# Second half of the memory gate's product in a float32 decoder layer: four of its eight weight pieces as seven block products each, with their sums on VectorE

## The reference

```python
h = rmsnorm(x, g_pre_mix[l])
proj = h @ w_in[l]
q_in, ckv, k_rope, lru_x, lru_y, gate_mla, gate_lru = jnp.split(proj, IN_SPLIT_IDX, axis=-1)
o_mla = mla_attention(q_in, ckv, k_rope, positions, g_ckv[l], w_ukv[l]) @ w_o_mla[l]
...
merged = jax.nn.sigmoid(gate_mla) * o_mla + jax.nn.sigmoid(gate_lru) * o_lru
```

## Time and profile before

| | |
|---|---|
| median of 3 runs | 1704.6 us (1704.03 to 1705.01) |
| the profiled execution's own time | 1704.42 us |
| its span, first to last instruction | 1702.6 us |
| TensorE matmul (PE) busy | 1694.0 us, 99%, 8887 matmuls |
| TensorE weight load (PEld) busy | 1453.7 us, 85% |
| VectorE (DVE) busy | 1293.3 us, 76% |
| ScalarE (ACT) busy | 980.3 us, 58% |
| GpSimd (POOL) busy | 266.5 us, 16% |
| chain that ended last | PE 97%, DVE 1%, ACT 1% |
| DMA | 375 MB, mean 220 GB/s |

### The profile page before, as it was taken

One profiled execution on the slowest core, in us unless ns is written; L12 is line 12 of the kernel. 1 busy time (PEld: TensorE's weight loads), 2 busy tenths in 40 slices (PEclk: granted clock), 3 DMA queues, 4 the chain that ended last, 5 costly groups with the idle time before them and its releaser, 6 DMA issues.

```text
span 1702.6 us, 24583 instructions
## 1 busy us (share of the span) xinstructions
PE 1694.0 (99%) x8887; PEld 1453.7 (85%) x8887; DVE 1293.3 (76%) x1638; ACT 980.3 (58%) x1238; POOL 266.5 (16%) x340
## 2 busy tenths in 40 slices
PE   9999999999999999999999999999999999999998
PEld 8888888888888888888888888888888888888887
DVE  7766675468788897676897687778877778977787
ACT  7656655454577766455556575556555555545564
POOL 0012212211365540002011101110001110001100
PEclk9999999999999999999999999999999999999999
DMA  9644459998678758499699856556765556765555
GB/s 346 204 132 149 152 188 293 316 268 237 177 221 232 234 175 301 133 368 274 234 302 255 220 198 196 183 184 208 253 199 178 181 195 212 236 201 191 197 187 203
DMA packets 230873, 375.07 MB, mean 220 GB/s; under 512 B 8720, under 2 KB 165008, under 8 KB 228752
## 3 DMA queue, kind: packets, MB, share of 16 engines
q1 hardware_dynamic: 210992, 326.66, 57.1%
q0 software_dynamic: 13888, 32.51, 9.4%
q10 hardware_dynamic: 5920, 14.94, 2.3%
HBM read 369.89 MB, written 36.70 MB: 239 GB/s over the span
## 4 chain that ended last, share of the span: by engine, by line
PE 97%; DVE 1%; ACT 1%; issue 1%; POOL 1%; DVEq 0%; ACTq 0%; POOLq 0%
PE ps L637 48%; PE ps L712 30%; PE ps L959 8%; PE ps L651 3%; PE ps L804 2%; PE ps L942 1%; PE ps L868 1%; PE ps L774 1%; PE ps L763 0%; ACT wsp L1629 0%; PE ps L744 0%; PE ps L897 0%; PE ps L873 0%; PE ps L1341 0%; PE ps L683 0%
## 5 line engine op out<-in xcount | busy, mean ns | idle before, releaser
L2010 DVE TENSOR_TENSOR wsp<-raw,wsp 128x2048 fp32r<-128x2048 f32 (+2 forms) x304 | 674.0, 2230 | 186.7 <-ACT wsp L1406 163.4
L1406 ACT ACTIVATE wsp<-raw 128x2048 fp32r<-128x2048 f32 (+2 forms) x274 | 502.1, 1843 | 126.4 <-PE ps L712 96.7
L637 PE MATMUL ps<-asp,wsp 128*128 128x512 f32 x3032 | 529.0, 336 | 0.0
L637 PEld LDWEIGHTS ps<-asp,wsp 128*128 128x128 f32 x3032 | 463.4, 188 | 62.8 <-DVE asp L2605 0.3
L712 PE MATMUL ps<-wsp,hsp 128*128 128x512 f32 x1536 | 354.0, 390 | 0.0
L712 PEld LDWEIGHTS ps<-wsp,hsp 128*128 128x128 f32 x1536 | 287.6, 188 | 59.7
L637 PE MATMUL ps<-hsp,wsp 128*128 128x512 f32 (+1 forms) x1744 | 314.1, 338 | 0.0
L637 PEld LDWEIGHTS ps<-hsp,wsp 128*128 128x128 f32 x1744 | 268.1, 188 | 36.7
L712 PE MATMUL ps<-wsp,asp 128*128 128x512 f32 x768 | 175.1, 389 | 0.0
L1417 ACT ACTIVATE cr<-ps 128x256 f32<-128x256 f32 x185 | 69.4, 380 | 180.9 <-PE ps L637 159.8
L712 PEld LDWEIGHTS ps<-wsp,asp 128*128 128x128 f32 x768 | 144.0, 188 | 29.8
(11 more groups left out here) (336 smaller groups left out, 1555.1 us busy)
## 6 DMA issues: line engine op xcount, KB each, us to landing
raw<-in_w_up SPq DMA_DIRECT2D x88, 1024.0 KB, 5.4
raw<-in_w_in SPq DMA_DIRECT2D x56, 1024.0 KB, 5.4
raw<-in_w_in SPq DMA_DIRECT2D x32, 768.0 KB, 4.5
raw<-in_w_down SPq DMA_DIRECT2D x24, 1024.0 KB, 5.4
sums<-in_w_down POOLq DMA_DIRECT2D x76, 256.0 KB, 7.5
raw<-in_w_o_mla SPq DMA_DIRECT2D x16, 1024.0 KB, 10.3
raw<-in_w_o_lru SPq DMA_DIRECT2D x16, 1024.0 KB, 6.1
raw<-sums SPq DMA_DIRECT2D x31, 512.0 KB, 3.9
```

Of the source, the lines that this page charges most:

```text
L637: mm = pe.matmul(ps[:, bank, 0:w], lhs(part, k), x[:, 0:w], start=(f and part == 0), stop=(l and part == 1))
L1406: act.activation(wsp[:, p0 % SLOTS, 0, 0:n], raw[:, p0 % SLOTS, 0:n], ACT.Copy).then_inc(hi_done, 1)
L2010: dve.tensor_tensor(wsp[:, slot, 1, 0:n], raw[:, slot, 0:n], wsp[:, slot, 0, 0:n].bitcast(F32), ALU.subtract).then_inc(lo_done, 1)
```

## The change

The second half becomes a phase of its own with twelve pieces (`GM_PLAN`): four plain ones as before (S0, S1, S6, S11), and four pairs "first", "made" for row blocks 8 to 15: (S2, S3), (S4, S5), (S7, S8), (S9, S10). A pair takes two row blocks k, k + 1 of 128 rows, both halves of the tokens and both halves of the columns, which is a 2 by 2 by 2 block product of eight block multiplications, and does it as seven (Winograd's form of Strassen's scheme). Seven by three terms are 21 matmuls of 128 x 512: 9 on "first", 12 on "made".

- SyncE loads the four weight blocks of a pair in three DMAs: two for "first" (768 KB), one of 256 KB for "made".
- VectorE makes the four weight sums of a pair itself (`gm_sums`, four additions of 128 x 512), then the low part of "first" (128 x 1536), later that of "made" (128 x 2048). ScalarE makes the high part of "made" only after the sums.
- The forms of h (four blocks of 128 x 128 for each pair, in `GM_FORMS`) are made in the first half: for each of G6, G7, S0, S1, VectorE runs `gm_form_sums` (one addition of 128 x 512, four operations of 128 x 128), ScalarE the high part (`gm_form_high`) and VectorE the low part (`gm_form_low`).
- The seven products gather in banks 0 to 3, the plain ones in banks 4 to 7. Behind the last pair ScalarE copies one bank out and VectorE does four operations (`gm_products`); after the last piece VectorE adds the four plain banks (`gm_plain`), and ScalarE takes the sigmoid in SBUF.
- TensorE waits for `gm_products` before M0, since M0 writes banks 0 to 3.

The diff, cut to what is spoken of:

```diff
+GM_PLAN = [("plain", 0), ("plain", 1), ("first", 4), ("made", 4),
+           ("first", 5), ("made", 5), ("plain", 2), ("first", 6),
+           ("made", 6), ("first", 7), ("made", 7), ("plain", 3)]
...
-PH_GM = Phase(PH_Q, 2, [0, 0, 0, 2] * 2, crosses=False)
+PH_GM = [Phase(PH_Q, 1, [0, 0, 0, 2] * 2, crosses=False)]
+PH_GM.append(Phase(PH_GM[0], 1, [0] * (len(GM_PLAN) - 1) + [4], crosses=False, twice=GM_FIRST))
...
 # TensorE
+                arrive(PH_GM[1], 0, c)
+                if c == GM_FIRST[0]:
+                    pe.wait_ge(tile_out, PH_GM[0].t_end)
+                if kind == "first":
+                    pe.wait_ge(gm_form_lo, GM_LO + pair - 4 + 1)
...
+                elif kind == "first":
+                    form_mm(q1, block(k0, 0), slot, 1, c == GM_FIRST[0], c == GM_FIRST[-1])
+                    form_mm(dn_plain_bank(1, 0, 1), block(k1, 0), slot, 3, False, False)
+                    mm = form_mm(dn_plain_bank(1, 0, 0), form(3), slot, 2, False, False)
+                else:
+                    first, last = c == GM_MADE[0], c == GM_MADE[-1]
+                    form_mm(q5, form(1), slot, 0, first, last)
+                    form_mm(q7, form(0), slot, 1, first, last)
+                    form_mm(q6, form(2), slot, 2, first, last)
+                    mm = form_mm(dn_plain_bank(1, 1, 1), block(k1, 1), slot, 3, False, False)
...
+            pe.wait_ge(gm_out, GM_OUT + 4)
             enter(PH_OM, [0, 1, 2, 3])
...
 # ScalarE
+            def gm_form_high(n):
+                act.wait_ge(gm_form_raw, GM_RAWS + n + 1)
+                act.activation(GM_FORMS[:, n, :, 0, :], GM_RAW.rearrange("p (f t) -> p f t", f=4), ACT.Copy).then_inc(gm_form_hi, 1)
             for c in range(4, 8):
-                hi(PH_GM, 0, c + LEAD)
+                hi(PH_GM[0], 0, c + LEAD)
+                gm_form_high(c - 4)
             gm_gates(0, 1)
...
 # VectorE
+            def gm_sums(ph, c):
+                first, made = (raw[:, (ph.p0 + at) % SLOTS, :] for at in (c, c + 1))
+                for at in (c, c + 1):
+                    dve.wait_ge(landed[(ph.p0 + at) % SLOTS], ph.landed(0, at))
+                own.mark(dve.tensor_tensor(made[:, 512:1024], made[:, 1536:2048], first[:, 1024:1536], ALU.add))
+                own.link(dve.tensor_tensor(made[:, 0:512], made[:, 1536:2048], first[:, 512:1024], ALU.add))
+                own.link(dve.tensor_tensor(made[:, 1024:1536], made[:, 0:512], first[:, 1024:1536], ALU.add))
+                dve.tensor_tensor(made[:, 1536:2048], made[:, 1024:1536], first[:, 1536:2048], ALU.add).then_inc(sums_made, 1)
...
             for c in range(4, 8):
-                lo(PH_GM, 0, c + LEAD)
+                lo(PH_GM[0], 0, c + LEAD)
+                if c > 4:
+                    gm_form_low(c - 5)
+                gm_form_sums(c - 4)
+            for c in range(LEAD, len(GM_PLAN) + LEAD):
+                if c in GM_FIRST:
+                    gm_sums(PH_GM[1], c)
+                    first_low(PH_GM[1], c)
+                else:
+                    lo(PH_GM[1], 0, c)
+                if c == LEAD:
+                    gm_form_low(3)
+                if c == GM_MADE[-1] + 2:
+                    gm_products()
+            gm_plain()
```

More of the change, by code:

```diff
@@ L76 @@
             ("plain", 4), ("first", 5), ("made", 5), ("first", 7), ("made", 7), ("plain", 6)]]
+GM_PLAN = [("plain", 0), ("plain", 1), ("first", 4), ("made", 4),
+           ("first", 5), ("made", 5), ("plain", 2), ("first", 6),
+           ("made", 6), ("first", 7), ("made", 7), ("plain", 3)]
+GM_FIRST, GM_MADE = ([c for c, (kind, _) in enumerate(GM_PLAN) if kind == name] for name in ("first", "made"))
 WO_PLAN = [("plain", pair) for pair in range(8)] + [
@@ L712, in rows_mm, with form_mm @@
                     mm = pe.matmul(ps[:, bank, :], src[:, k, low * T + m * P:low * T + (m + 1) * P], wsp[:, c, part, cols],
+                                   start=(first and t == 0), stop=(last and t == 2))
+                return mm
+            def form_mm(bank, lhs, slot, block, first, last):
+                for t, (part, low) in enumerate(TERMS):
+                    mm = pe.matmul(ps[:, bank, :], lhs(low), wsp[:, slot, part, quarter(block)],
                                    start=(first and t == 0), stop=(last and t == 2))
@@ L918, in _ @@
+            for c in range(len(GM_PLAN)):
+                gm_piece(c)
+            for b in gm_banks:
+                last_in.pop(b, None)
+            pe.wait_ge(gm_out, GM_OUT + 4)
             enter(PH_OM, [0, 1, 2, 3])
@@ L955, in turn_merged @@
                     turn(a_tok, k, 4 + k // 2 % 4, (k % 2) * T, m_turned)
-            def form_mm(bank, lhs, slot, block, first, last):
-                for t, (part, low) in enumerate(TERMS):
-                    mm = pe.matmul(ps[:, bank, :], lhs(low), wsp[:, slot, part, quarter(block)],
-                                   start=(first and t == 0), stop=(last and t == 2))
-                return mm
             def gl_half(h):
@@ L2215, in _, with gm_plain @@
+            def gm_plain():
+                dve.wait_ge(gm_out, GM_OUT + 4)
+                for n in range(4):
+                    dve.wait_ge(gemm_step, PH_GM[1].g(0, PH_GM[1].done[n]))
+                    dve.tensor_tensor(gm_res(n), gm_res(n), ps[:, 4 + n, :], ALU.add).then_inc(gm_out, 1)
+            attention(HEADS // 2 - 1, PH_GM[0], 0, lambda part: None)
             e_, s_, s2, p_ = st[:, 48:64], st[:, 32:48], st[:, 64:80], st[:, 80:96]
```

155 lines of the change are left out of this document (114 added, 41 removed).

## The result

The changed kernel takes 1717.22 us, the median of five executions (1715.55 to 1719.5); the kernel before, beside it, 1704.6 (1704.03 to 1705.01). The ratio is 1.0075, with a 95% interval of 1.0063 to 1.0086: slower by 12.6 us. Forecast were 1712.5 and at most 1715.0. The sign was right, and the time came out above the range.

The account below looks back on a forecast made before the run. The prediction took TensorE to bound the kernel. Against the profiled 1704.42 us it summed -2.72 (matmuls saved) + 9.49 (waits for low parts) + 1.31 (S11's load) = +8.08, so 1712.5 us, range 1708.7 to 1715.0.

Parts of the forecast that it names:

- Removed work: Second half on TensorE: 60 block products in place of 64, 12 matmuls fewer, 2.72 us saved.
- The handshake in the first half: ScalarE and VectorE wait on each other over the forms: rounds of 7.20 us; S0, S1, S2 late by 1.66, 1.76, 2.01.
- The rival in which it doesn't bind: First half: the lead of 7.9 us covers the form work, only the pairs count; 1703.2 us, chance 0.09.
- The pairs: Second half: VectorE takes 6.93 us per pair, TensorE 4.76; waits at S3, S4, S5, S9, S10 of 0.55 to 1.61 us.
- The load of S11: DMA of S11's weights, slowed beside GpSimd's additions, lands at 334.6, so TensorE begins S11 late: +1.31 us.
- the first rival: S11's load is in time, as GpSimd's additions may run earlier; all else as forecast: 1711.2 us, chance 0.25.
- S8's load: Other loads of the stage were said to have 1 us or more in hand, this one the least.
- The step that failed: End of the second half: four adds and sigmoids behind S11 cost nothing, hidden by M0 and M1 (10.9 us of TensorE).
- The rival of 1718: TensorE's clock falls to 1.2 GHz at each of the three longest waits, 6 us more; chance 0.03.

Follow-up runs that it names:

- e6: e3, with GpSimd's second batch of weight sums in DRAM held until S10's matmuls are done: 1703.37 us, ratio 0.9993; repeated in another series, 1703.34 us.
- e4: The kernel before, with only the forms made in its first half in the change's order and used by nobody: 1712.38 us, ratio 1.0047.
- e2: The changed kernel, with each form's high part one place later on ScalarE, behind the next piece's high part: 1710.77 us, ratio 1.0038.
- e3: The changed kernel with the edits of e1 and e2 together: 1705.76 us, ratio 1.0005.
- e1: The changed kernel, with M0's first turn on TensorE no longer waiting for the second half's sigmoids: 1713.45 us, ratio 1.0053.
- e8: The kernel before, with one wait added: TensorE begins S1 only after the low part of S3: 1706.95 us, ratio 1.0016.

## Why the prediction was right and wrong

**Removed work: right.** 12 matmuls fewer, 2.72 us. In e6, where two small waits are left, M0 begins 1.4 us earlier: by the pace 0.56 us are lost at S9, 0.65 at S10 (both with the restart) and 0.13 behind it, and 2.72 - 1.34 = 1.38.

**The handshake in the first half: right, and it decides.** Forecast were low parts 7.20 us apart. The timeline of VectorE in the changed kernel:

```profile
285.20 2.29 DVE L2098 TENSOR_TENSOR wsp<-raw,wsp 128x2048 fp32r<-128x2048 f32 x1 [2.50 <-ACT wsp L1479]
...
292.38 2.29 DVE L2098 TENSOR_TENSOR wsp<-raw,wsp 128x2048 fp32r<-128x2048 f32 x1 [2.50 <-ACT wsp L1479]
...
299.57 2.29 DVE L2098 TENSOR_TENSOR wsp<-raw,wsp 128x2048 fp32r<-128x2048 f32 x1 [2.50 <-ACT wsp L1479]
```

And that of ScalarE:

```profile
289.92 0.63 ACT L1638 ACTIVATE gm_forms<-cr 128x512 fp32r<-128x512 f32 x1 [4.74 <-DVE cr L2331]
```

The low parts stand 7.18 and 7.19 apart. In each round VectorE waits 2.50 us for ScalarE, and ScalarE 4.74 for VectorE. e4 shows the cause without the rest of the change, and e2 removes it by an order alone. The rival in which it doesn't bind (1703.2) fell; e6's 1703.4 is its number, but by another order. A slip in the forecast's working: 192 matmuls are 43.6 us and not 43.5 (65.41 x 192 / 288), which puts S0's wait at 1.76 in place of 1.66; measured were 1.74. Another, without effect: the earlier trace rows leave out a wait of PEld of 1.5 us for `ident`, so 0.7 was not the longest in the kernel.

**The pairs: right.** 6.93 us forecast for each on VectorE, against TensorE's 4.76; from one "made" low part to the next it takes 7.0, and the waits at S3 to S5 and S10 came out within 0.1 us.

**The load of S11: wrong, and made up for by chance.** "I take 334.6" gave 1.31 us at S11; S11 lost 0.12. The additions of GpSimd were over earlier than before, as the first rival allowed: its next ones were issued at 327.99 in place of 336.13, and S11's load, issued at 326.76, took 5.0 us. Instead the weights of S7 came late for VectorE:

```profile
322.32 0.69 DVE L2314 TENSOR_TENSOR raw<-raw 128x512 f32<-128x512 f32 x1 [0.87 <-DMA raw<-in_w_in]
```

So S9 gained 1.55 in place of 0.55. (ScalarE waited 1.38 us for S9's weights too, but VectorE came to that piece only 2 us later, so this cost nothing.) The forecast had S8's load as the one with the least in hand. That loads beside the additions take twice as long was right (10.8 against 5.0 in e3 and e6); which load is hit was not. The sum came within 0.1 us by two errors that cancel.

**The step that failed** is this sentence: "The four adds and sigmoids behind S11 are hidden by M0 and M1, which are ready". The weights were ready; the count of free banks wasn't. In `token_piece` TensorE waits for `tile_out` ahead of M0, and I followed only the low parts and the products. So a term stood at nothing that measured 3.15 us, and e1 shows it: with that wait gone, M0 follows S11 at once. The right reckoning was in reach from the forecast's own numbers: products to 344.2, low part of M1 to 346.4, one add (0.61 behind it), one sigmoid (about 0.7, as the gates of the earlier trace rows) and the restart (0.17) give 347.9 for M0 instead of 344.5. That is +3.4, measured 3.15. With it the forecast would have been 1715.9, above the stated range even without the clock.

**The clock: wrong by its chance.** The rival of 1718 had a chance of 0.03, and three of five executions are within 1.5 us of it, though by another sum. It came from the earlier trace rows, where PE is nearly idle and the granted clock stays at 1.00. That is true in the changed kernel as well, in the pause itself (1.00 and 0.99); the half clock shows from the end of the pause on, when TensorE works again without a break, and the earlier trace rows have no such stretch. So they could say little for or against. The Trainium skill ("TensorE: Matmul & The Clock Gate", "HAM oscillation") describes matmul bursts broken by waits that start at the half clock again; the windows above agree, with 0.50 for 3.4 and 6.8 us, and so does e8 with one wait of 2.4 us. They differ in that a fall does not come every time, as S0, S1 and e4 show. Of the three falls that I priced at 6 us, the one at S2 was free, because TensorE wasn't the bound there, those at S0 and S1 didn't occur in the profiled execution, and one came at a wait that I hadn't seen.

## What to carry to other kernels

Reckon a round trip wherever two engines that work in order pass small steps to each other: if one's next large step stands behind the other's answer, both lose their lead, and a change of order gives it back for nothing. When work is moved past the end of a stage, follow every counter that the next stage's first instruction waits for, the release of its buffers too, not only its data. And in a kernel that TensorE bounds, price a stall of 2 us or more at up to twice its length, unless another engine is the bound right behind it: here 2.40 us of idle time cost 4.05 with the fall (e8), and the 3.15 of M0 cost 6.13.

## What was not expected of the hardware

- The half clock comes in some executions and not in others of one kernel. With one wait of 2.4 us, four of eleven executions were some 2 us longer (e8); with three waits of up to 2.8 us, e4's profiled execution had a mean clock of 0.999 and no fall.
- The fall begins near the end of the wait: in the changed kernel the clock is 1.00 while TensorE stands, then 0.50, from 0.2 us after S2's begin and from 0.65 us before M0's. In e3 it begins 0.95 us after M0's. Behind waits of 1.8 to 2.4 us it lasted 3.4 us, at the 3.0 of the changed kernel's M0 and the 5.84 of e2's 6.8. Why it is twice as long there stays open.
- GpSimd's additions in DRAM move only 1.05 MB in 15 us (316 to 331 in e3), yet beside them four loads of 1 MB take 10.8 us each in the median, in place of the 5.0 of e6. How so little traffic does this stays open.
